# Modulation matmuls move from the delta rule's first stage into the HGRN levels, and some constant matmuls leave those levels

## What is computed

```
for l in range(2):
    sh1, sc1, g1, sh2, sc2, g2 = split(silu(c) @ w_ada[l] + b_ada[l], 6)     # w_ada[l]: 1024 x 6144, for c and for c_ctx
    h = rms_norm(x) * (1 + sc1) + sh1
    y = concat(delta_rule(h), latent_attention(h), hgrn(h)) @ w_out[l]
    x = x + g1 * rms_norm(y)
    h = rms_norm(x) * (1 + sc2) + sh2
    x = x + g2 * rms_norm(relu(h @ w1) ** 2 @ w2)
```

## Time and profile before

| | |
|---|---|
| median of three executions | 2367.18 us (2364.3 to 2369.07) |
| profiled execution | 2368.38 us, its span 2366.5 us |
| mean granted PE clock | 0.991 |
| PE, DVE, ACT busy over the span | 2270.2, 1174.8, 863.1 us |
| first stage of the delta rule | 172 to 214 us in layer 0, 1476 to 1516 us in layer 1 |
| HGRN levels and first update | 487 to 571 us in layer 0, about 1766 to 1824 us in layer 1 |

### The profile page before, as it was taken

One profiled execution on the slowest core, in us unless ns is written; L12 is line 12 of the kernel. 1 busy time (PEld: TensorE's weight loads), 2 busy tenths in 40 slices (PEclk: granted clock), 3 DMA queues, 4 the chain that ended last, 5 costly groups with the idle time before them and its releaser, 6 DMA issues.

```text
span 2366.5 us, 43250 instructions
## 1 busy us (share of the span) xinstructions
PE 2270.2 (96%) x19374; PEld 1829.4 (77%) x19374; DVE 1174.8 (50%) x1848; ACT 863.1 (36%) x1250; POOL 219.5 (9%) x204
## 2 busy tenths in 40 slices
PE   7999899999999999999999999989999999999998
PEld 5876598876668788888888677658785669888887
DVE  4674353187363551424233577436249456444443
ACT  5362134224453421222213536233323455322233
POOL 3013410000120100000000011321000111000000
PEclk9999999999999999999999999999999999999999
DMA  8218101134301121212212221810212302323222
GB/s 316 63 57 267 48 22 57 56 111 135 118 1 37 36 89 54 72 57 69 66 59 72 89 63 54 272 53 19 72 55 68 119 5 68 107 89 107 90 89 71
DMA packets 161695, 198.44 MB, mean 84 GB/s; under 512 B 18358, under 2 KB 129432, under 8 KB 160871
## 3 DMA queue, kind: packets, MB, share of 16 engines
q1 hardware_dynamic: 155536, 185.20, 24.3%
q10 hardware_dynamic: 5271, 10.10, 1.2%
q0 software_dynamic: 704, 0.37, 0.2%
HBM read 184.60 MB, written 11.06 MB: 83 GB/s over the span
## 4 chain that ended last, share of the span: by engine, by line
PE 86%; DVE 5%; ACT 4%; issue 2%; SPq 1%; DMA 1%; POOL 0%; DVEq 0%; ACTq 0%
PE ps L1525 35%; PE ps L840 16%; PE ps L1443 5%; PE ps L1057 3%; PE ps L1387 2%; PE ps L933 2%; PE ps L1482 2%; PE ps L1196 1%; PE ps L818 1%; PE ps L874 1%; PE ps L1214 1%; PE ps L827 1%; PE ps L1400 1%; PE ps L1417 1%; PE ps L1018 1%
## 5 line engine op out<-in xcount | busy, mean ns | idle before, releaser
L1525 PE MATMUL ps<-region_r 128*128 128x512 f32 (+1 forms) x1536 | 376.9, 354 | 0.0
L1525 PEld LDWEIGHTS ps<-region_r 128*128 128x128 f32 x1536 | 270.6, 188 | 40.5
L1525 PE MATMUL ps<-region_r,weights_r 128*128 128x512 f32 (+1 forms) x768 | 229.8, 354 | 0.0
L2130 DVE TENSOR_TENSOR weights_r<-weights,region_r 128x2048 fp32r<-128x2048 f32 x62 | 141.9, 2288 | 120.2 <-ACT region_r L1661 120.2
L1525 PE MATMUL ps<-mixed_r,weights_r 128*128 128x512 f32 (+1 forms) x672 | 201.1, 354 | 0.0
L1525 PE MATMUL ps<-modulated_r,region_r 128*128 128x256 f32 (+1 forms) x624 | 186.9, 354 | 0.0
L1525 PE MATMUL ps<-mixed_r,region_r 128*128 128x256 f32 (+1 forms) x624 | 186.7, 354 | 0.0
L1525 PEld LDWEIGHTS ps<-region_r,weights_r 128*128 128x128 f32 x768 | 144.5, 188 | 20.5
L2059 ACT ACTIVATE region<-ps,cst 128x768 f32<-128x768 f32 (+1 forms) x64 | 50.3, 796 | 298.4 <-PE ps L1525 280.5
L2633 DVE TENSOR_TENSOR region_r<-region 128x768 fp32r<-128x768 f32 (+1 forms) x64 | 52.8, 824 | 201.3 <-ACT region L2059 201.3
L1525 PEld LDWEIGHTS ps<-mixed_r,weights_r 128*128 128x128 f32 x672 | 126.4, 188 | 18.1
(11 more groups left out here) (421 smaller groups left out, 4727.4 us busy)
## 6 DMA issues: line engine op xcount, KB each, us to landing
weights<-in_w_mlp SPq DMA_DIRECT2D x64, 1024.0 KB, 5.6
weights<-in_w_ada SPq DMA_DIRECT2D x40, 1024.0 KB, 5.2
weights<-in_w_in SPq DMA_DIRECT2D x34, 1024.0 KB, 5.2
region<-in_w_ada SPq DMA_DIRECT2D x8, 1024.0 KB, 17.5
weights<-in_w_out SPq DMA_DIRECT2D x8, 1024.0 KB, 6.5
x_kept<-residual SPq DMA_DIRECT2D x2, 3072.0 KB, 12.7
region<-decays_kept ACTq DMA_DIRECT2D x4, 1536.0 KB, 11.5
residual<-x_kept SPq DMA_DIRECT2D x2, 3072.0 KB, 11.0
```

The costliest lines, as they stand in the source:

```text
L1525: last = mm(dst[:, CTX + a:CTX + b], w[:, k, m], r[:, a:b], start=(k == 0 and r is r_low), stop=(k == KB - 1 and w is low))
L2130: v.tensor_tensor(ring_r[:, at, :], ring[:, at, :], mlp_high(j), ALU.subtract).then_inc(w_low_ready, 1)
```

## The change

Two groups of layer 0 and four of layer 1 move from the delta rule's first stage into the HGRN levels of the same layer. Layer 0 has then four groups in the first stage and eight in the levels, layer 1 two and six. `ada_items(l)` lists the items behind which a half stands: the last pair of levels 0 and 1, then the items from level 2 on (in layer 0 all of them but (2,0), in layer 1 all). ACT copies a group one item after the item of its second half. Layer 0's levels lose their constants, and in layer 1 the first pair has one ahead of a product where it had four. The bias of the moved columns and the gain A2, which needs them, are done after HGRN. The order of `LOADS` follows.

```diff
-ADA_GDN, ADA_HGRN = (6, 6), (6, 2)
-ADA_GDN_AT, ADA_HGRN_AT = (0, 24), (12, 36)
+ADA_GDN, ADA_HGRN = (4, 2), (8, 6)
+ADA_GDN_AT, ADA_HGRN_AT = (0, 24), (8, 28)
...
+        def ada_items(l):
+
+            n, points = len(pairs_out(l)), 2 * ADA_HGRN[l]
+            later = [(lv, j) for lv in range(2, NLEV) for j in range(n)]
+            while len(later) > points - 2:
+                full = [lv for lv in range(2, NLEV) if sum(a == lv for a, _ in later) == max(sum(b == k for b, _ in later) for k in range(2, NLEV))][0]
+                later.remove(min(item_of for item_of in later if item_of[0] == full))
+            return [(0, n - 1), (1, n - 1)] + later
...
-                    ada_point(first + 2 * ci, first)
+                    if ci < ADA_GDN[l]:
+                        ada_point(first + 2 * ci, first)
...
-                LEVEL_HOLDS, HOLDS_FROM = ((1, 1, 1), (4, 1)), (5, 2)
+                LEVEL_HOLDS, HOLDS_FROM = ((0, 0, 0), (1, 1)), (5, 2)
...
-                        if lv < 2 and p == pairs[-1]:
-                            ada_point(ADA_HGRN_AT[l] + lv, ADA_HGRN_AT[l])
-                        elif 2 <= lv and 2 * lv <= points and p in pairs[-2:]:
-                            ada_point(ADA_HGRN_AT[l] + 2 * lv - 2 + (p == pairs[-1]), ADA_HGRN_AT[l])
+                        if (lv, j) in ada_items(l):
+                            ada_point(ADA_HGRN_AT[l] + ada_items(l).index((lv, j)), ADA_HGRN_AT[l])
...
-                    ada_group(ADA_GDN_AT[l] + 2 * ci)
+                    if ci < ADA_GDN[l]:
+                        ada_group(ADA_GDN_AT[l] + 2 * ci)
...
+                items = [(lv, j) for lv in range(NLEV) for j in range(len(pairs))]
+                group_after = [items[min(items.index(at) + 1, len(items) - 1)] for at in ada_items(l)[1::2]]
                 for lv in range(NLEV):
                     for j in range(len(pairs)):
                         keep_keys(lv, j)
                         if j == 0 and lv in (1, 2):
                             gate_unit(lv - 1)
-                    if 1 <= lv <= ADA_HGRN[l]:
-                        ada_group(ADA_HGRN_AT[l] + 2 * lv - 2)
+                        if (lv, j) in group_after:
+                            ada_group(ADA_HGRN_AT[l] + 2 * group_after.index((lv, j)))
...
-                add_bias(l, 16, 40, ps[:, 7, 0:48])
-                v.tensor_copy(cst[:, 5:6], mods[:, l, 39, 0:1]).then_inc(ada_read, 1)
+                late = 16 + 4 * ADA_GDN[l]
+                add_bias(l, 16, late, ps[:, 7, 0:2 * (late - 16)])
+                v.tensor_copy(cst[:, 5:6], mods[:, l, late - 1, 0:1]).then_inc(ada_read, 1)
...
-                gain(A2, 32, V_MLPPRE, True)
...
-                add_bias(l, 40, 48, ps[:, 7, 0:16])
+                add_bias(l, late, 48, ps[:, 7, 0:2 * (48 - late)])
...
+                gain(A2, 32, V_MLPPRE, True)
```

More of the change, by code:

```diff
@@ L1029, in _ @@
                         pe.wait_ge(rows_copied, l + 1)
-                    ada_point(first + 2 * ci + 1, first)
+                    if ci < ADA_GDN[l]:
+                        ada_point(first + 2 * ci + 1, first)
                 def token_rows(i):
@@ L1198, in value_unit @@
                     last.then_inc(gemm_out, 1)
-                pairs, points = pairs_out(l), 2 * ADA_HGRN[l]
+                pairs = pairs_out(l)
                 def gate_step(u, k):
@@ L2542, in _ @@
                 dve.wait_ge(ada_tr, ADA_FIRST + ADA_HGRN_AT[l] // 2 + ADA_HGRN[l])
-                add_bias(l, 40, 48, ps[:, 7, 0:16])
+                add_bias(l, late, 48, ps[:, 7, 0:2 * (48 - late)])
                 if l == 0:
-                    add_bias(1, 0, 16, ps[:, 7, 16:48])
+                    add_bias(1, 0, 16, ps[:, 7, 2 * (48 - late):2 * (48 - late) + 32])
                 v.tensor_copy(cst[:, 5:6], mods[:, l, 47, 0:1]).then_inc(ada_read, 1)
+                gain(A2, 32, V_MLPPRE, True)
                 link(gain(G2, 40, V_MLPPOST, False))
```

## The result

After the change the kernel takes 2376.8 us (median of 9 executions, 2372.7 to 2384.3), before it 2369.1 beside it (9 executions, 2364.3 to 2371.9). The ratio is 1.0037, 95% interval 1.0026 to 1.0048: slower by 7.7 us where 3.1 faster was forecast, and outside the predicted range. The profiled execution took 2374.5 us with a span of 2372.6, 6.1 more than before.

The account below looks back on a forecast made before the run. PE was taken to bound the delta rule's first stage and DVE the levels. The terms -3.3 - 9.3 + 6.5 + 3.0 = -3.1 us led from the median 2367.2 to 2364.1 us, range 2355 to 2371.

Parts of the forecast that it names:

- the gains at the gates: After the first stages: gates start at 210.4 instead of 214.37 in layer 0, 1506.9 instead of 1516.26 in layer 1.
- the wait for ACT's copy: Layer 1's levels: PE's half (5,0) stands 4.6 us for a group copy queued behind level 4's spreading.
- +6.5: Layer 1's levels: first update 6.9 us late, taken as 6.5 slower, with ends of 0 and 9.
- -3.3 + 3.0: Layer 0: first stage gains 3.3 us after a low-clock cost of 0.7; its levels lose 3.0.
- Together the two stages give 12.6 us: First stages of both layers: gains of 3.3 and 9.3 us; 11 if DVE's chunks lengthen by 0.3 each.
- At nothing: Later bias and gain A2, first-stage copies and loads, layer 1's later attention loads: costed at zero, at most 5 us per load.
- the pause of 2.32 us: Layer 0's levels before the change: a PE "issue" pause in mid-product that nothing in the trace ends.
- Levels, layer 0: Layer 0's levels: after a wait at half (5,0), first update comes 3.2 us late, taken as 3.0.
- The term's end of 5: Layer 0's levels, upper end: 14 loads of 1 MB at 3.2 us each need 45 us, all these levels have.
- Hidden levels: Rival, chance 0.25: levels cost 0 to 2 us, so the 12.6 us gain stands, about 2355.5 us.
- Less from the first stage: Rival, chance 0.12: POOL or ACT also limits the chunks, half of the 12.6 us stays away, 2370 us.
- The low clock: Rival, chance 0.13: clock stays low through layer 1's chain of updates, 8 us more in all, 2372 us.

Follow-up runs that it names:

- Layer 1 alone: Before with the change made in layer 1 only, layer 0 keeping its groups, constants and order of copies: 2366.6 us, ratio 0.9995.
- small matmuls: The change in layer 0 only, with 24 and 46 small matmuls ahead of the first stages to keep PE's instruction places of before: 2374.2 us, ratio 1.0027.
- short loads: Layer 0's level loads cut from 1 MB to 256 KB: against after 2370.5 us; against layer 0 alone with small matmuls 2372.1 us.
- layer 0 alone: Before with the change made in layer 0 only, layer 1 keeping its groups, constants and order of copies: 2377.5 us, ratio 1.0041.
- after, shifted: After with 32 more matmuls of 32 columns ahead of layer 0's decay rows: 2379.2 us, ratio 1.0050.
- stage alone: Before with the moved groups left out altogether, levels, constants and copies kept: 2365.4 us, ratio 0.9988.
- constants back: After with the constants of before put back in both layers' levels: 2380.7 us, ratio 1.0050.
- copy first: After with ACT's copy of the group that ends in level 4 moved ahead of that level's spreading, both layers: 2368.6 us, ratio 1.0008.
- copies moved and stream kept: Layer 1 alone with both ACT copies moved, plus 48 small matmuls ahead of layer 1's first stage: 2367.2 us, ratio 0.9992.
- stage alone and stream kept: Stage alone plus 24 small matmuls ahead of layer 0's first stage and 48 ahead of layer 1's: 2361.1 us, ratio 0.9967.

## Why the prediction was wrong

**Right.** PE bounds the stage, DVE is next, and the gains at the gates (forecast 4.0 and 9.3, measured 4.4 and 9.6). In layer 1 the wait for ACT's copy, the low clock behind it and the late wide copies are there, and moving the two copies takes 5.1 us off. Their price of +6.5 agrees with the 6.8 of the two profiled executions by luck: over all traces layer 1's levels take some 8.4 us longer (an estimate from the means, 68.6 us in five traces against 60.1 in eight). Layer 1 alone gives -2.1 (-3.3 to +0.7) where -2.8 was forecast.

**Wrong: layer 0, where -3.3 + 3.0 was forecast and +8.7 measured.** By the medians that sum has three parts. 6.2 us go when the small matmuls restore the place of what follows in PE's stream (8.7 less 2.5). 2.2 go with the short loads (2.5 less 0.3). What is left is +0.3 for the terms that I did reckon, which gave -0.3. The intervals are 2.5 to 3 us to either side, so that this agreement is no proof and neither the sizes nor the order of the first two parts is shown; with the stream shifted, in after itself, short loads gave 4.9. Nor is all of the 6.2 shown to be the shift. The two profiled executions lie 4.9 us apart, 7.6 without the small matmuls, and 4.9 of these stand in layer 0's chain of updates: it ran at a clock of 0.73 with layer 0 alone and at 1.00 with the stream kept, but at 1.00 in after too, whose layer 0 is the same program as in layer 0 alone:

```profile
576.00:594.00 18.00, 18.00 (x225) 17.93 (x226) 12.88 (x41) 6.04 (x9) 0.00 (x0) 1.00 0.01 2
```

What many traces do show is the gate stage: from the gate's first matmul to the corner layer 0 takes 82.7 to 87.7 us in the seven traces with fewer groups there and nothing put in their place, 80.4 to 83.0 in the three with the stream kept, and 80.2 to 82.8 in the four with the program of before. By the medians and means that is some 2 to 3 of the 4.4 us won at the gate (an estimate). In after, shifted, with 32 matmuls more ahead, it takes 77.7.

**The step that failed** is the sum itself: it carries the stages' gain to the end ("Together the two stages give 12.6 us") and puts all else under "At nothing". The stage alone, which puts no work into the levels, brought 3.3 us of the 12.6 (0.7 to 4.7). Taking instructions out of PE's stream ahead of a stage of small matmuls moves every later instruction against the 16 KB loads, and with the count restored 10.9 us came through: 7.6 us, some 3 to either side, were lost that way. That the pauses are these loads is shown; that the shift is all of the loss is not, since in layer 1 restoring the place made the kernel slower. I had the pause of 2.32 us before me, took it for a mark of layer 0's levels, and priced it only as an end of a range.

A second miss, smaller than the ledger's 6.2 us, is the size of "Levels, layer 0": 3.0 was taken, and the levels take 83.1 to 86.1 us in five traces of the change against 78.4 to 82.6 in the four with before's layer 0, some 4 us more (an estimate from the means, 84.7 and 80.5). The wait that the term was reckoned from is not there in after: half (5,0) of layer 0 follows its product at once (552.05), and what stands in its place are a half that waits 2.94 us for its load (523.11) and pauses for instructions, 3.75 us in product (5,0). ACT's wait appears only when the loads are short. The term's end of 5 was reckoned from the loads' own time, not from either.

**The rivals.** Hidden levels: no, layer 1's waits are there. Less from the first stage: not at the gates, but the effect that it describes came one stage later and for another reason. The low clock: partly. The mean granted clock of an execution is 0.991 before and 0.985 after (nine executions, 0.979 to 0.989, the two slowest of 2384.3 us at 0.982 and 0.979). With the constants back it is 0.988 and the kernel is no faster, so the clock alone is not the loss. In after PE's clock is 0.86 over the levels' end (1804 to 1829) and over the updates (1829 to 1841) in layer 1, and the chain of updates lost 1.7 us; with layer 0 alone, layer 0's updates ran at 0.73 and lost 4.9:

```profile
571.00:590.00 19.00, 19.00 (x142) 18.93 (x144) 7.93 (x35) 7.51 (x11) 0.00 (x0) 0.73 0.00 1
```

PE is busy throughout this window, and just ahead of it (566 to 571) the clock was 1.00: it can also fall and stay low while PE works. By the rule of the Trainium skill cited with that rival ("TensorE: Matmul & The Clock Gate", section "HAM oscillation — how this bites in real kernels") PE comes back cold after each wait. Half (5,0) of layer 1 did, after 5.42 us; with copy first the longest wait left there is 1.67 us and the clock stays at 1.00.

**Open** is why layer 1's gate stage lost 7.1 us in one run and 3.0 in another with its instructions at the same place in the stream (copies moved and stream kept, stage alone and stream kept); the clock was 0.73 and 0.88 in 1505 to 1530. So it is open, too, whether the place of the loads or something that differs from execution to execution decides there. That the loads' place can be chosen for a gain is not shown: the shift gave after 3.7 us, within the intervals, and cost before 4.4.

## What to carry to other kernels

An edit that takes instructions out of one engine's stream moves all that follow against the blocks in which they are loaded; among this kernel's small matmuls that was worth as much as the edit. Compare with a kernel that keeps the count (small matmuls in place of what went) before believing or dropping an idea, and look for "issue" pauses in stages that the edit doesn't touch. Don't put a stage's microseconds down to an edit from one execution: here the same program differed by up to 7.5 us at one point. In an engine's in-order queue a copy that another engine waits for belongs ahead of work that itself has to wait, and a copy that nobody waits for belongs behind work that does hold up the end.

## What the runs showed of the hardware that was not expected

PE's instructions come in loads of 16 KB over a DMA queue of their own, about 1 us each (0.88 to 2.2 us in before and after), at least 3.27 us apart there, and PE goes on 1.24 to 1.58 us after one lands. Pauses from this are up to 4.43 us long (after, shifted, at 1522.80). 32 matmuls of 32 rows cost 1.0 us, 32 with 128 rows of the same 32 columns 7.1 to 7.5. Adding 1.0 us of empty work made the kernel 5.4 us slower (1.7 to 7.8). With layer 0 alone the granted clock fell from 1.00 (566 to 571) to 0.50, 1.2 of 2.4 GHz (576 to 581), while PE was busy without a break from 571 on.
